# Expert layer on one Trainium2 core: selection of the first group ahead of the expert order, eight fixed places, place products between gate and up

## What is computed

```python
g_idx = top_k(softmax(t @ w_group_router + b_group_router), 1)     # 1 of 4 groups
e_val, e_idx = top_k(softmax(logits of that group's 8 experts), 2) # 2 experts per token
weights = g_val * e_val / sum(e_val)
for e in range(32):
    hid = silu(t @ w_gate[e]) * (t @ w_up[e])
    out = out + combine[:, e:e+1] * (hid @ w_down[e])
```

## Time and profile before

| | us |
|---|---|
| median of 3 runs | 473.38 |
| lowest and highest of them | 471.88, 474.62 |
| the profiled execution: its time | 471.33 |
| its span (first to last instruction) | 469.6 |
| PE busy in the span | 415.7 (89%) |
| DVE busy | 236.2 (50%) |
| ACT busy | 190.7 (41%) |
| DMA, hardware queue | 142.96 MB, 80.5% of 16 engines' span |

### The profile page before, as it was taken

One profiled execution on the slowest core, in us unless ns is written; L12 is line 12 of the kernel. 1 busy time (PEld: TensorE's weight loads), 2 busy tenths in 40 slices (PEclk: granted clock), 3 DMA queues, 4 the chain that ended last, 5 costly groups with the idle time before them and its releaser, 6 DMA issues.

```text
span 469.6 us, 9066 instructions
## 1 busy us (share of the span) xinstructions
PE 415.7 (89%) x3550; PEld 337.4 (72%) x3550; DVE 236.2 (50%) x528; ACT 190.7 (41%) x282; POOL 158.0 (34%) x106
## 2 busy tenths in 40 slices
PE   7999999999998999999989999974806999859783
PEld 6999999998998999999967565542303655526541
DVE  2579999999999945784386212210100122102014
ACT  4674556749986769444254121120100211201004
POOL 7579898882999983008000000000000000000000
PEclk9999999999999999999999999998857999979887
DMA  8886877652665477559794999999999999999972
GB/s 279 275 264 201 277 275 277 232 180 91 170 202 168 135 265 278 193 194 372 302 412 176 402 426 397 402 421 414 419 417 415 415 420 416 420 410 423 415 289 91
DMA packets 61618, 143.55 MB, mean 306 GB/s; under 512 B 5204, under 2 KB 44124, under 8 KB 53384
## 3 DMA queue, kind: packets, MB, share of 16 engines
q1 hardware_dynamic: 61560, 142.96, 80.5%
q10 hardware_dynamic: 16, 0.00, 0.0%
HBM read 141.91 MB, written 1.05 MB: 304 GB/s over the span
## 4 chain that ended last, share of the span: by engine, by line
PE 59%; SPq 20%; DMA 11%; issue 4%; DVE 3%; ACT 1%; DVEq 0%
PE ps L1318 14%; PE ps L1316 14%; PE ps L1317 14%; SPq L420 8%; SPq L424 6%; PE ps L1537 6%; SPq L442 5%; DMA ring<-in_w_up 4%; DMA ring<-in_w_down 4%; PE ps L1579 3%; DMA ring<-in_w_in 2%; PE ps L1513 2%; PE ps L1488 2%; PE ps L1307 2%; PE ps L1362 2%
## 5 line engine op out<-in xcount | busy, mean ns | idle before, releaser
L581 POOL TENSOR_TENSOR ring_r<-ring,ring_r 128x1024 fp32r<-128x1024 f32 x58 | 146.7, 2559 | 59.0 <-ACT ring_r L623 59.0
L1537 PE MATMUL ps<-ring,xslot 128*32 128x256 f32 (+1 forms) x832 | 74.3, 430 | 36.7 <-DMA ring<-in_w_gate 22.4
L1316 PE MATMUL ps<-u_hi,ring_r 128*128 128x256 f32 x368 | 104.1, 283 | 1.5 <-ACT gateB L631 0.9
L1318 PE MATMUL ps<-u_hi,ring_r 128*128 128x256 f32 x368 | 104.1, 283 | 0.0
L1317 PE MATMUL ps<-u_lo,ring_r 128*128 128x256 f32 x368 | 103.5, 281 | 0.0
L943 DVE SCALAR_TENSOR_TENSOR ps<-cpad,par,ps 128x256 f32<-128x256 f32 x232 | 92.0, 480 | 1.1 <-ACT ps L650 1.1
L1537 PEld LDWEIGHTS ps<-ring,xslot 128*32 128x32 f32 (+1 forms) x832 | 42.3, 130 | 64.6 <-issue 43.1
L623 ACT ACTIVATE ring_r<-ring 128x2048 fp32r<-128x2048 f32 x35 | 66.9, 1910 | 19.9 <-DMA ring<-in_w_rnn_out 9.7
L1316 PEld LDWEIGHTS ps<-u_hi,ring_r 128*128 128x128 f32 x368 | 69.4, 189 | 2.1 <-ACT gateB L631 1.3
L1317 PEld LDWEIGHTS ps<-u_lo,ring_r 128*128 128x128 f32 x368 | 69.6, 189 | 0.0
L1318 PEld LDWEIGHTS ps<-u_hi,ring_r 128*128 128x128 f32 x368 | 68.9, 187 | 0.0
(11 more groups left out here) (266 smaller groups left out, 695.1 us busy)
## 6 DMA issues: line engine op xcount, KB each, us to landing
ring<-in_w_gate SPq DMA_DIRECT2D x28, 1024.0 KB, 13.5
ring<-in_w_in SPq DMA_DIRECT2D x24, 1024.0 KB, 5.4
ring<-in_w_up SPq DMA_DIRECT2D x24, 1024.0 KB, 17.7
ring<-in_w_down SPq DMA_DIRECT2D x40, 512.0 KB, 17.9
ring_high<-in_w_up SPq DMA_DIRECT2D x8, 1024.0 KB, 15.7
extra<-in_w_down SPq DMA_DIRECT2D x16, 512.0 KB, 13.7
ring<-in_w_rnn_out SPq DMA_DIRECT2D x4, 1024.0 KB, 5.0
ring<-in_w_conf_out SPq DMA_DIRECT2D x4, 1024.0 KB, 4.9
```

The costliest lines, as they stand in the source:

```text
L581: gp.tensor_tensor(ring_r[:, MIX_SLOT + k % SEG, cols], ring[:, MIX_SLOT + k % SEG, cols], ring_r[:, HI_SLOT + k % SEG, cols].bitcast(F32) ...
L1316: pe.matmul(dst, w_hi(k), x_hi(k), start=(k == 0), stop=False)
L1318: last = pe.matmul(dst, w_lo(k), x_hi(k), start=False, stop=(k == KC - 1))
L1537: last = pe.matmul(ps[width * j:width * (j + 1), 4, part * FE:(part + 1) * FE], xslot[:, k, pair * P + j * width:pair * P + (j + 1) * widt ...
```

## The change

1. `FIXED` is 8 instead of 6: experts 0 to 7 lie at places 0 to 7, so all of units 0 to 11 are known beforehand. SP waits for `dve_order` before unit 12 instead of before unit 9, and loads no numbers for units 9 to 11.
2. On DVE, `fill_sel` of group 0 and the two last halves of `hn_lo` stand ahead of the place chain instead of behind it. The four softmax instructions stand ahead of the wait for the place products; everything else that reads them stays behind it.
3. On TensorE, the place products move from ahead of the first gather to between the gate and the up products of the first half of group 0. They write to PSUM bank 5 instead of bank 7.
4. ScalarE's wait in the first step is for the rank transposes and the round count instead of for `rankT`.

```diff
-FIXED = 6
-RANK_PLACES = [(0, 6), (20, 24), (6, 20), (24, 32)]
-NARROW_FIXED = slice(4, 6)
+FIXED = 8
+RANK_PLACES = [(0, 8), (20, 24), (8, 20), (24, 32)]
+NARROW_FIXED = slice(4, 8)
...
+FIXED_UNITS = FIXED // QUAD * QUAD_UNITS
...
+        order_ps = ps[0:1, 5, NE:2 * NE]
+        ranks_ps = ps[:, 5, 2 * NE:4 * NE]
+        rankT_ps = ps[0:NE, 5, 4 * NE:4 * NE + T]
...
-            sp.wait_ge(dve_order, 1)
             for n in range(RING, SPAN_UNITS):
-                experts = [placed(e) for e in unit_places(n)]
+                if n == FIXED_UNITS:
+                    sp.wait_ge(dve_order, 1)
+                experts = unit_places(n) if n < FIXED_UNITS else [placed(e) for e in unit_places(n)]
                 place_free(0, n)
                 load_unit(n, experts=experts)
...
                     if u == 0:
-                        act.wait_ge(dve_rankT, 1)
+                        act.wait_ge(pe_rankT, 1)
+                        act.wait_ge(rounds_ready, 1)
...
+            fill_sel(0, rt[:, 9, :, :]).then_inc(dve_sel, 1)
+            hn_low(0, 1)
+            hn_low(1, 1)
 
             counts = ps[:, 6, 2 * NE:3 * NE]
...
             v.tensor_scalar(place[:, 2, :], place_d[:, :], place_c[:, 2:3], None, ALU.is_equal).then_inc(dve_place, 1)
...
-            fill_sel(0, rt[:, 9, :, :]).then_inc(dve_sel, 1)
-            hn_low(0, 1)
-            hn_low(1, 1)
...
             v.tensor_copy(rounds[:, :], stat[:, 13:14]).then_inc(rounds_ready, 1)
 
-            v.wait_ge(pe_place, 1)
-            v.tensor_copy(order_e[:, :], ps[0:1, 7, T:T + NE]).then_inc(dve_order, 1)
...
             link(v.tensor_tensor(stat[:, 14:16], stat[:, 12:14], stat[:, 2:4], ALU.mult))
+
+            v.wait_ge(pe_place, 1)
+            v.tensor_copy(order_e[:, :], order_ps).then_inc(dve_order, 1)
...
-            pe.wait_ge(dve_place, 1)
-            pe.wait_ge(dve_rankT0, 1)
-            pe.matmul(ps[0:1, 7, T:T + NE], place_k[:, 0:1], place[:, 2, :], start=True, stop=True)
...
+            def place_ranks():
+                pe.wait_ge(dve_place, 1)
+                pe.wait_ge(dve_rankT0, 1)
+                pe.matmul(order_ps, place_k[:, 0:1], place[:, 2, :], start=True, stop=True)
+                for tc in range(TC):
+                    pe.matmul(ranks_ps[:, tc * NE:(tc + 1) * NE], rankT0[:, tc * P:(tc + 1) * P],
+                              place[:, 2, :], start=True, stop=True)
+                pe.matmul(rankT_ps, place[:, 2, :], rankT0[:, :], start=True, stop=True).then_inc(pe_place, 1)
...
                         last.then_inc((pe_gu_half, pe_gu)[part], count // 2)
+                        if u == pair == part == 0:
+                            place_ranks()
```

More of the change, by code:

```diff
@@ L1114, in _, with fill_sel @@
                                    op0=ALU.mult, op1=ALU.add).then_inc(dve_rank, 1)
+            def fill_sel(u, ranks):
+                first, n = group_places(u)
+                for tc in range(TC):
+                    ins = v.tensor_tensor(
+                        sel[:, tc, :].rearrange("p (e s) -> p e s", e=n),
+                        bcast(ranks[:, tc, first:first + n].rearrange("p (e a) -> p e a", a=1), 2, 2 * P // n),
+                        bcast(iota_s[:, 0:2 * P // n].rearrange("p (a s) -> p a s", a=1), 1, n), ALU.is_equal)
+                return ins
+            fill_sel(0, rt[:, 9, :, :]).then_inc(dve_sel, 1)
+            hn_low(0, 1)
+            hn_low(1, 1)
             counts = ps[:, 6, 2 * NE:3 * NE]
@@ L1127, in _ @@
             v.tensor_scalar(place[:, 2, :], place_d[:, :], place_c[:, 2:3], None, ALU.is_equal).then_inc(dve_place, 1)
-            def fill_sel(u, ranks):
-                first, n = group_places(u)
-                for tc in range(TC):
-                    ins = v.tensor_tensor(
-                        sel[:, tc, :].rearrange("p (e s) -> p e s", e=n),
-                        bcast(ranks[:, tc, first:first + n].rearrange("p (e a) -> p e a", a=1), 2, 2 * P // n),
-                        bcast(iota_s[:, 0:2 * P // n].rearrange("p (a s) -> p a s", a=1), 1, n), ALU.is_equal)
-                return ins
-            fill_sel(0, rt[:, 9, :, :]).then_inc(dve_sel, 1)
-            hn_low(0, 1)
-            hn_low(1, 1)
             over = rt[:, 6:10, :, :].rearrange("p a t e -> p (a t) e")[:, 0:MAX_ROUNDS - 1, :]
@@ L1180, in _ @@
             link(v.tensor_tensor(stat[:, 14:16], stat[:, 12:14], stat[:, 2:4], ALU.mult))
+            v.wait_ge(pe_place, 1)
+            v.tensor_copy(order_e[:, :], order_ps).then_inc(dve_order, 1)
+            step(v.tensor_scalar(secondT[:, :], rankT_ps, SECOND - 0.5, -SECOND, ALU.is_gt, ALU.mult))
+            ranks2 = ranks_ps.rearrange("p (t e) -> p t e", t=TC)
+            link(v.tensor_scalar(rt[:, 11, :, :], ranks2, SECOND - 0.5, None, ALU.is_gt))
+            link(v.scalar_tensor_tensor(out=rank[:, :, 0:NE], in0=rt[:, 11, :, :], scalar=-SECOND, in1=ranks2,
+                                        op0=ALU.mult, op1=ALU.add))
+            v.tensor_tensor(rankT[:, :], secondT[:, :], rankT_ps, ALU.add).then_inc(dve_rankT, 1)
+            step(v.tensor_scalar(rank[:, :, NE:], rank[:, :, 0:QUAD], -float(SLOTS), None, ALU.add))
+            link(v.tensor_scalar(rt[:, 10, :, :], rank[:, :, 0:NE], 0.5, None, ALU.is_gt))
+            link(v.tensor_tensor(rt[:, 5, :, :], rt[:, 10, :, :], rt[:, 11, :, :], ALU.subtract))
             link(v.tensor_tensor(rt[:, 5, :, :], rt[:, 5, :, :], bcast(col(12), 2, NE), ALU.mult))
```

## The result

The changed kernel takes 474.76 us (median of 20 executions), the kernel before 472.59 in the same number: a ratio of 1.0048, 95% interval 1.0031 to 1.0066, so 2.3 us slower (1.5 to 3.1). The forecast shift was 1.6 us.

What follows compares the result with a forecast made beforehand. TensorE's chain up to 295.4, then weight transfers, bound the kernel. The gather's 1.6 us gain shrinks to 0.3 at up; a 1.9 us stall makes the weights' product 1.6 late, put on 473.38: 475.0, range 472.5 to 477.0.

Steps and rivals of the forecast that it cites:

- forecast shift: Whole kernel: the end comes 1.6 us later, as the first weights' product does; bounds +1.2 to +2.3.
- TensorE's chain up to unit 17 sets the end: Expert stage up to 295.4: TensorE's products set when unit 17 is issued; a microsecond there is one at the end.
- The gather starts 1.6 earlier: TensorE's first gather: waiting for DVE's selection only, it starts at 245.2 instead of 246.78, 1.6 us earlier.
- Place products hold up the stream by 1.24: TensorE, between gate and up: the four place products delay the up product by 1.24 us.
- the bounds (0.9 and 1.65): Limits in us on the place products' delay of the up product; they move the end by -0.4 and +0.4.
- DVE's chain of 5.35 behind the place products: DVE, from the place products to y_lo's end: 5.35 us, ending at 259.5, so TensorE stands 1.9 us.
- the spare time of 2.2 us: Kernel before: DVE's first y_lo was expected ready at 255.67, 2.2 us ahead of TensorE's need.
- The register load stays in series: DVE's round-count load before y_lo stays in the 1.26 us gap; rival, it hides: +0.6, 474.0, chance 0.10.
- The transfers: Weight transfers: unit 9 runs 1.6 us earlier, unit 10 0.3 earlier, then idle; from unit 11 on 1.6 later.
- The earlier restart doesn't count: Weight stream: unit 9's earlier issue gains nothing; rival, it takes 1.6 us off: 471.8, 0.07 together with a no-stall case.
- The clock: Rival: TensorE's clock falls in the 1.9 us stall before the first weights' product, costing 2.95 more: 477.9, chance 0.08.
- The number: Forecast time of the changed kernel: 475.0 us, the shift put on the three-run median 473.38.

Runs made afterwards that it cites:

- e8: e1 without the five warming products on TensorE ahead of the gather; 0.9965 of the kernel before, 470.28 us.
- e4: The changed kernel with five useless DVE instructions added ahead of the first y_lo; 1.0097 of the kernel before.
- e3: The kernel before with five useless DVE instructions added behind the combined weights, ahead of the first y_lo; 0.9995 of the kernel before.
- e6: The changed kernel with DVE's register load of the round count moved ahead of its wait for the place products; 1.0000 of the kernel before.
- e1: The changed kernel with DVE's first y_lo moved ahead of its wait for the place products; 0.9967 of the kernel before.
- e5: The changed kernel with 8 warming products on TensorE in front of its wait for y_lo, the wait kept; 1.0040 of the kernel before.
- e9: The changed kernel itself, unedited, in three more profiled executions; 476.8, 473.31 and 474.18 us.
- e7: The kernel before with only the eight fixed places and SP's later wait for the order; 0.9999 of the kernel before.

## Why the prediction was right, point by point

- *TensorE's chain up to unit 17 sets the end.* Right: the table above, over 5.8 us from e8 to e4. The rest of the way was not tested by an experiment, but the traces bear it out: in the twelve profiled executions whose last down products wait for the last transfer, it is 161.1 to 163.7 us from unit 17's issue to these products, with no order by the chain. This spread of 2.6 us also says why one execution can't show an effect of 1.6.
- *The gather starts 1.6 earlier.* Right: 244.01 + 0.92 is 244.9, 1.85 earlier by the timeline; the products that follow run as computed.
- *Place products hold up the stream by 1.24.* Right: 1.25 between 251.60 and 252.85, no bubble at either side, so the bounds (0.9 and 1.65) were wider than needed.
- *DVE's chain of 5.35 behind the place products.* Right: 253.02 to 258.38 is 5.36, and the stall 1.92 for the 1.9 forecast. The shift of the weights' product by timelines is 258.44 + 0.92 - 257.84 = 1.52, against 1.6. e3 and e4 show the spare time of 2.2 and its loss.
- *The register load stays in series.* Right: 1.03 of "issue" again, and only e6, which moves it in the program, takes it out of DVE's chain. Its price, 0.6 left of 1.6, was near too: 0.50. The page "Perfetto Trace Analysis" of the Trainium skill, by which the load could have run ahead during the wait (section "DVE / Act Engine Instruction"), is not borne out by these rows.
- *The transfers.* Right: restart early, idle again behind unit 10 (0 GB/s in 265 to 266), later by the chain from unit 11 on.
- *The earlier restart doesn't count.* Right for the changed kernel, which is slower for all its earlier restart. e1 has the restart too, and its chain gains 0.36 (forecast without a stall: 0.3); its time alone would not decide, as said there.
- *The clock.* The step that came out wrong. The rival was given 0.08 and 2.95 us, because TensorE had kept its clock in a window with 0.34 of 2 us busy and lost it after 6.2 us of idle; from these two I took an idle of 1.9 to be harmless. It was so in two profiled executions of four only; in the other two the clock fell and cost 1.5 us, not 2.95. The trace of the kernel before had closer rows, which the prediction didn't read. TensorE's timeline shows that the window of the earlier trace rows cuts into an idle of 2.87 us (granted 1.00 in 316 to 318), and that two shorter ones, of 2.08 and 2.04, did cost the clock (granted 0.50 in 438 to 440 and in 448 to 450): the 64 products behind each took 5.35 us instead of 3.66, 1.7 more.

```profile
315.66 3.66 PE L1537 MATMUL ps<-ring,xslot 128*32 128x256 f32 x64 [2.87 <-DMA ring<-in_w_gate]
435.94 5.35 PE L1537 MATMUL ps<-ring,xslot 128*32 128x256 f32 x64 [2.08 <-DMA ring<-in_w_gate]
446.21 5.35 PE L1537 MATMUL ps<-ring,xslot 128*32 128x256 f32 x64 [2.04 <-DMA ring<-in_w_up]
```

  One stretch that kept its clock doesn't show that the next one like it will, and here the price could have been read too. The forecast and this rival are two cases of one kernel. 1.5 plus half of 1.5 would make the 2.3 measured and so the 0.7 us by which the forecast shift was too small. That this is where the 0.7 comes from is not shown: 1.6 is still inside the interval of 1.5 to 3.1, and the end of the execution varies by as much (last section).
- *The number.* 475.0 against 474.76 is closer than its terms, and that is luck. The base, a median of 3 runs, was 473.38, 0.8 above the 472.59 of 20 runs; the shift was 0.7 below the one measured; the two nearly cancel. From the base of 20 runs the forecast would have been 474.2.

## What to carry to other kernels

Moving products off the front of a chain moves the release of everything that hangs on them: follow that work, in its engine's order, to the next place where the first engine waits, and count the spare time it had there; here 2.2 us of spare became a stall of 1.9. Look for instructions whose inputs are long ready but which are now queued behind the new wait, and put them ahead of it (e1 moves one such instruction); the same goes for scalar work such as a register load (e6). Price a new stall on TensorE with the clock that may fall behind it, as a chance and not as yes or no, from all stalls of about that length in the trace at hand and not from one.

## What the runs showed of the hardware

TensorE's granted clock stays at 1.00 during an idle of 1.92 us, and falls to 0.50 some 0.5 us behind its end, for about 3.4 us, in two profiled executions of four with the same instructions; with fillers in the idle time it did not fall (e5), nor behind 0.92 us of idle (e6), one execution each. Behind 3.76 us of idle (e4) it fell only near 265.2, 1.7 us after work had begun again at 263.59. In the kernel before, it stayed up behind 2.87 us and fell behind 2.08 and 2.04. So in these rows the length of the idle alone doesn't decide; what does stays open.

The executions also differ at the end, where no edit reached. The last down products wait 1.08 us for the last transfer in the kernel before and then take 1.97 us; in the profiled execution of the changed one they wait 2.28 and take 3.58, at a granted clock of 0.50:

```profile
457.44 1.97 PE ps L1579 x16
```

```profile
460.46 3.58 PE ps L1586 x16
```

```profile
461.00:462.00 1.00, 1.00 (x8) 0.20 (x4) 0.00 (x0) 0.00 (x0) 0.00 (x0) 0.50 0.00 0
```

In e9 they take 3.31, 2.96 and 1.97. These 1.6 us are as much as the forecast change itself, and another reason why single executions don't show it. The time outside the span varies too: 1.73 us in the profiled execution of the kernel before, 1.71 to 3.33 in all runs. Whether the change makes this fall more frequent, and so adds to the 2.3 us, was not tested; it is no matter of the changed kernel alone, since e5 has it too, and e7 (3.01 us), which keeps the old order on TensorE and DVE.
